# Activations and memory that arrive transposed, at the start of a fused two-block transformer kernel

## The reference

```python
def first_block(x, mem, positions, ...):
    cos, sin = rope_tables(positions, x.dtype)
    mem_n = rmsnorm(mem, g_mem)
    h = rmsnorm(x, g_mix_pre)
    proj = h @ w_in                     # 1024 x 2048
    q, k = proj[..., :512], proj[..., 512:1024]
    v, u = proj[..., 1024:1536], proj[..., 1536:]
    q, k = apply_partial_rope(q, cos, sin), apply_partial_rope(k, cos, sin)
    ...
    pooled = causal_multiscale_pool(u)
    po = jnp.einsum('bsgc,gcd->bsgd', pooled, w_pool) * pool_scale
    ...
    kv = mem_n @ w_xkv                  # cross attention's keys and values

def rmsnorm(x, g):
    return x * lax.rsqrt(jnp.mean(x * x, axis=-1, keepdims=True) + EPS) * g
```

## Time and profile before

| | |
|---|---|
| median of three runs | 1021.13 us (1020.99 to 1021.32) |
| the profiled execution | 1022.37 us, its span 1019.8 us |
| TensorE busy | 1008.9 us, 99% of the span |
| VectorE, ScalarE, GpSimd busy | 761.3 us (75%), 539.2 us (53%), 31.8 us (3%) |
| chain that ended last | TensorE 99%, ScalarE 1% |
| DMA | 183.41 MB, mean 180 GB/s; in the first 45 us some 420 GB/s |

### The profile page before, as it was taken

The page is one execution under the profiler, slowest core; times in us unless marked ns, Lnnn a source line. Parts: engine busy times, 40 slices in busy tenths (PEclk is TensorE's granted clock), DMA queues, the critical chain, the costliest instruction groups (busy, mean ns, idle before and its releaser), DMA issues.

```text
span 1019.8 us, 17235 instructions
## 1 busy us (share of the span) xinstructions
PE 1008.9 (99%) x6914; PEld 905.6 (89%) x6914; DVE 761.3 (75%) x1041; ACT 539.2 (53%) x757; POOL 31.8 (3%) x49
## 2 busy tenths in 40 slices
PE   8999999999999999999999999999999999999997
PEld 7999899898888889998888888889999988888885
DVE  6888587698887457897788888447788869888632
ACT  6876485574544346865464544336534365454431
POOL 1100000000000001000000000001000100000000
PEclk9999999999999999999999999999999999999999
DMA  9833554266555546443345555555434237555521
GB/s 342 349 135 134 197 198 152 86 226 209 205 185 188 204 165 269 176 157 126 125 165 206 203 177 197 206 181 208 166 130 166 84 129 248 201 197 178 201 83 42
DMA packets 27293, 183.41 MB, mean 180 GB/s; under 512 B 3200, under 2 KB 3472, under 8 KB 6112
## 3 DMA queue, kind: packets, MB, share of 16 engines
q1 hardware_dynamic: 25056, 175.01, 48.0%
q0 software_dynamic: 1744, 7.16, 1.9%
q10 hardware_dynamic: 432, 0.37, 0.1%
HBM read 181.48 MB, written 1.05 MB: 179 GB/s over the span
## 4 chain that ended last, share of the span: by engine, by line
PE 99%; ACT 1%; DVE 0%; issue 0%; ACTq 0%
PE GT L1918 11%; PE D L1918 11%; PE GT L1881 10%; PE GT L1882 9%; PE GT L1883 9%; PE D L1881 8%; PE D L1883 8%; PE D L1882 8%; PE GT L1924 6%; PE D L1924 5%; PE D L2652 1%; PE GT L2088 1%; PE GT L2146 1%; PE D L2510 1%; PE GT L2525 1%; PE GT L2107 1%
## 5 line engine op out<-in xcount | busy, mean ns | idle before, releaser
L1033 DVE TENSOR_TENSOR s_wlo<-s_raw,s_whi 128x2048 fp32r<-128x2048 f32 (+1 forms) x164 | 355.5, 2170 | 97.4 <-ACT s_whi L516 95.8
L516 ACT ACTIVATE s_whi<-s_raw 128x2048 fp32r<-128x2048 f32 (+1 forms) x164 | 298.0, 1820 | 140.5 <-PE D L1883 86.1
L1918 PE MATMUL GT<-s_x,s_whi 128*128 128x512 f32 x512 | 124.4, 390 | 0.0
L1918 PE MATMUL D<-s_x,s_whi 128*128 128x512 f32 x480 | 116.4, 390 | 0.0
L1918 PEld LDWEIGHTS GT<-s_x,s_whi 128*128 128x128 f32 x512 | 93.6, 188 | 17.3
L1881 PE MATMUL D<-s_whi,s_hTh 128*128 128x512 f32 x264 | 103.0, 390 | 0.0
L1883 PE MATMUL D<-s_whi,s_hTl 128*128 128x512 f32 x264 | 102.7, 389 | 0.0
L1882 PE MATMUL D<-s_wlo,s_hTh 128*128 128x512 f32 x264 | 102.7, 389 | 0.0
L1918 PEld LDWEIGHTS D<-s_x,s_whi 128*128 128x128 f32 x480 | 87.8, 188 | 16.3
L1881 PE MATMUL GT<-s_x,s_whi 128*128 128x256 f32 x336 | 94.6, 282 | 0.0
L1883 PE MATMUL GT<-s_x,s_wlo 128*128 128x256 f32 x336 | 93.4, 278 | 0.0
(11 more groups left out here) (409 smaller groups left out, 1788.6 us busy)
## 6 DMA issues: line engine op xcount, KB each, us to landing
s_raw<-in_stream SPq DMA_DIRECT2D x164, 1024.0 KB, 4.8
s_gb<-in_rows POOLq DMA_DIRECT2D x4, 512.0 KB, 4.1
s_xn<-in_x SPq DMA_DIRECT2D x2, 512.0 KB, 4.6
s_raw<-in_stream SPq DMA_DIRECT2D x4, 256.0 KB, 6.6
s_y<-in_mem POOLq DMA_DIRECT2D x1, 1024.0 KB, 10.2
s_w<-in_cmpw POOLq DMA_DIRECT2D x1, 1024.0 KB, 10.9
s_poolm<-in_poolm POOLq DMA_DIRECT2D x1, 768.0 KB, 12.1
s_retd<-in_retm POOLq DMA_DIRECT2D x1, 768.0 KB, 5.2
```

The source lines that it names most:

```text
L516: nc.scalar.activation(high(u, n), raw[:, u % RING, 0:n], ACT.Copy)\
L1033: nc.vector.tensor_tensor(low(u, n), raw[:, u % RING, 0:n], high(u, n), ALU.subtract)\
L1918: return nc.tensor.matmul(o[:, f, :], high_block(u, kt, f), x2[:, kt, :], start=start, stop=stop)
```

## The change

x and the memory are given to the program a second time, transposed and laid out as the kernel needs them (`xT`, `memT`: feature on the partition, eight blocks of 256 tokens). The natural ones are still loaded, for the squares and the residual.

- SP's queue: x transposed in three pieces (two blocks, two blocks, four blocks of features), each followed by the part of unit 0 that belongs to it; then unit 1 in two halves, unit 2, the constants in one piece, natural x, unit 3. ScalarE's queue loads only the gains.
- `raw_transposes` is gone: ScalarE and VectorE read the loaded `xraw` (it lies in `y`). One copy on ScalarE of one column of the cleared tile stands ahead. The squares of x move behind the split of unit 2.
- `early_unit` serves units 1, 2 and 3; unit 1 can begin on its first half. Units 2 and 3 are accumulated in banks D0 and D1. The spread of rstd (two matmuls) moves from behind unit 1 to behind unit 3.
- GpSimd: the memory goes into `vx`, and `memT`, one more MB, into `y`, when the high part of unit 3 is ready (before: of unit 4).
- `mem_transposes` is replaced by `mem_rstd`: two matmuls that spread the memory's rstd. VectorE multiplies `memT` by it, now after the low part of unit 8 instead of ahead of the tables.
- The angles are reduced once; the cosine is taken as the sine of pi/2 less the size of the reduced angle.

```diff
+PIECES = ((0, 1), (1, 2), (2, 4))
+PIECE_OF = (0, 1, 2, 2)
...
+        xraw = y[:].rearrange("p t n -> p (t n)").rearrange("p (k n) -> p k n", k=KT)
+        memT = y[:].rearrange("p t (k n) -> p (t k) n", n=S)
+            return (G[0], G[1], DB[0], DB[1])[u]
...
-            for t in range(NT):
-                sp.dma_start(xn[:, t, :], x_in[t * P:(t + 1) * P, :]).then_inc(sem(f"x_in{t}"), 16)
-            for i in range(4):
-                sp.dma_start(raw[:, 0, 512 * i:512 * i + 512], stream[0, :, 512 * i:512 * i + 512])\
+            for i, (a, b) in enumerate(PIECES):
+                sp.dma_start(xraw[:, 2 * a:2 * b, :], xT_in[:, 2 * a:2 * b, :]).then_inc(sem(f"xT_in{i}"), 16)
+                sp.dma_start(raw[:, 0, 512 * a:512 * b], stream[0, :, 512 * a:512 * b])\
                     .then_inc(sem(f"first_in{i}"), 16)
             for j in range(1, RING):
-                sp.dma_start(raw[:, j, :], stream[j, :, :]).then_inc(landed[j], 16)
+                if j == 3:
+                    for t in range(NT):
+                        sp.dma_start(xn[:, t, :], x_in[t * P:(t + 1) * P, :]).then_inc(sem("x_in"), 16)
                 if j == 1:
-                    sp.dma_start(cst[:, CONST_FIRST:], consts_in[:, CONST_FIRST:]).then_inc(sem("cst_in"), 16)
+                    sp.dma_start(raw[:, 1, 0:UNIT // 2], stream[1, :, 0:UNIT // 2]).then_inc(sem("second_in"), 16)
+                    sp.dma_start(raw[:, 1, UNIT // 2:UNIT], stream[1, :, UNIT // 2:UNIT]).then_inc(landed[1], 16)
+                else:
+                    sp.dma_start(raw[:, j, :], stream[j, :, :]).then_inc(landed[j], 16)
+                if j == 2:
+                    sp.dma_start(cst[:], consts_in).then_inc(sem("cst_in"), 16)
...
-            power("x0.0")
-            power("x0.1")
-
-            pool.wait_ge(sem("norm_sq"), 4)
-            pool.wait_ge(hi_ready, 5)
-            pool.dma_start(y[:], mem_in.rearrange("(t p) d -> p t d", p=P)).then_inc(sem("mem_in"), 16)
-            pool.dma_start(poolm[:], poolm_in).then_inc(sem("poolm_in"), 16)
-            pool.dma_start(wpool, wpool_in).then_inc(sem("wpool_in"), 16)
+            pool.wait_ge(sem("cst_in"), 16)
+            power("x0.0")
+            power("x0.1")
+
+            pool.wait_ge(hi_ready, 4)
+            pool.dma_start(vx[:], mem_in.rearrange("(t p) d -> p t d", p=P)).then_inc(sem("mem_in"), 16)
+            pool.dma_start(memT[:], memT_in).then_inc(sem("memT_in"), 16)
+            pool.dma_start(poolm[:], poolm_in).then_inc(sem("pool_in"), 16)
+            pool.dma_start(wpool, wpool_in).then_inc(sem("pool_in"), 16)
+            pool.wait_ge(unit_done, 1)
             pool.dma_start(gb[:], rows_in[0, :].partition_broadcast(P)).then_inc(sem("gb_in"), 16)
...
+            def mem_hi():
+
+                for kt in range(KT):
+                    if kt % 4 == 0:
+                        act.wait_ge(sem("mem_scaled"), kt // 4 + 1)
+                    nc.scalar.activation(memTh[:, kt, :], memT[:, kt, :], ACT.Copy, scale=gain("g_mem", kt))\
+                        .then_inc(sem("norm_hi"), 1)
...
-            norm_squares(0, xn, lambda c: chunk(y, c), parts=range(2))
+            act.wait_ge(sem("warm_in"), 1)
+            nc.scalar.activation(small[:, 0:1], gb[:, 0:1], ACT.Copy)
             for i in range(4):
-                norm_hi(0, xTh, (2 * i, 2 * i + 1))
-                act.wait_ge(sem(f"first_in{i}"), 16)
+                act.wait_ge(sem(f"xT_in{PIECE_OF[i]}"), 16)
+                for kt in (2 * i, 2 * i + 1):
+                    nc.scalar.activation(xTh[:, kt, :], xraw[:, kt, :], ACT.Copy, scale=gain("g_mix_pre", kt))\
+                        .then_inc(sem("norm_hi"), 1)
+                act.wait_ge(sem(f"first_in{PIECE_OF[i]}"), 16)
                 nc.scalar.activation(whi[:, 0, 512 * i:512 * i + 512], raw[:, 0, 512 * i:512 * i + 512],
                                      ACT.Copy).then_inc(sem("first_hi") if i < 3 else hi_ready, 1)
-            for j in range(1, 4):
-                split(j)
+            act.wait_ge(sem("second_in"), 16)
+            nc.scalar.activation(whi[:, 1, 0:UNIT // 2], raw[:, 1, 0:UNIT // 2], ACT.Copy).then_inc(sem("first_hi"), 1)
+            act.wait_ge(landed[1], 16)
+            nc.scalar.activation(whi[:, 1, UNIT // 2:UNIT], raw[:, 1, UNIT // 2:UNIT], ACT.Copy).then_inc(hi_ready, 1)
+            split(2)
+            norm_squares(0, xn, lambda c: x_scratch[:, c, :], parts=range(2))
+            split(3)
...
             act.wait_ge(sem("mem_in"), 16)
-            mem_scratch = kxT[:].rearrange("p (c k) n -> p c (k n)", c=4)
-            norm_squares(1, y, lambda c: mem_scratch[:, c, :])
+            norm_squares(1, vx, lambda c: x_scratch[:, c, :])
...
-            norm_hi(1, memTh)
+            mem_hi()
...
-            def mem_scaled(t):
-
-                dve.wait_ge(rstd_ready, pow_at(f"mem.{t}") + 1)
-                nc.vector.tensor_scalar(y[:, t, :], y[:, t, :], rstd[:, POW_COL[f"mem.{t}"]], None, ALU.mult)\
+            def mem_scaled(b):
+
+                if b == 0:
+                    dve.wait_ge(sem("memT_in"), 16)
+                    dve.wait_ge(sem("norm_tr"), 4)
+                part = memT[:, 4 * b:4 * b + 4, :]
+                nc.vector.tensor_tensor(part, part, same_rows(DB[2][:, 0:S], 4), ALU.mult)\
                     .then_inc(sem("mem_scaled"), 1)
+            def mem_lo():
...
+                    nc.vector.scalar_tensor_tensor(memTl[:, kt, :], memT[:, kt, :], gain("g_mem", kt), memTh[:, kt, :],
+                                                   ALU.mult, ALU.subtract).then_inc(sem("xT_ready"), 1)
...
-            dve.wait_ge(sem("x_in1"), 16)
             dve.wait_ge(sem("gains_in"), 16)
             for i in range(4):
-                norm_lo(0, xTh, xTl, (2 * i, 2 * i + 1))
+                dve.wait_ge(sem(f"xT_in{PIECE_OF[i]}"), 16)
+                dve.wait_ge(sem("norm_hi"), 2 * i + 2)
+                for kt in (2 * i, 2 * i + 1):
+                    nc.vector.scalar_tensor_tensor(xTl[:, kt, :], xraw[:, kt, :], gain("g_mix_pre", kt),
+                                                   xTh[:, kt, :], ALU.mult, ALU.subtract)\
+                        .then_inc(sem("xT_ready"), 1)
...
+            dve.wait_ge(sem("x_in"), 32)
...
-            angle(sinT, 0.0, 0.0)
+            link(nc.vector.tensor_scalar(turns, ang, 1.0 / two_pi, magic, ALU.mult, ALU.add))
+            link(nc.vector.tensor_scalar(turns, turns, -magic, None, ALU.add))
+            for c in (c1, c2, c3):
+                link(nc.vector.scalar_tensor_tensor(ang, turns, -c, ang, ALU.mult, ALU.add))
+            link(nc.vector.tensor_scalar(sinT[:], ang, 3.1415925, -3.1415925, ALU.min, ALU.max))
+            link(nc.vector.scalar_tensor_tensor(cosT[:], sinT[:], -1.0, sinT[:], ALU.mult, ALU.max))
+            nc.vector.tensor_scalar(cosT[:], cosT[:], math.pi / 2, None, ALU.subtract).then_inc(sem("angles"), 1)
...
-            dve.wait_ge(sem("angles"), 1)
-            angle(cosT, math.pi / 2, 0.25)
             norm_mean(1, "mem", 0)
             norm_mean(1, "mem", 1)
-            mem_scaled(0)
-            mem_scaled(1)
...
                 split(u0 + 4 + j + RING)
+                if j == 0:
+                    mem_scaled(0)
+                    mem_scaled(1)
                 if j == 1:
-                    norm_lo(1, memTh, memTl)
+                    mem_lo()
...
-            def second_unit(u):
+            def early_unit(u):
 
                 hi, lo = (w(u).rearrange("p (k n) -> p k n", k=KT) for w in (high, low))
-                o = G[bank(u)]
-                pe.wait_ge(hi_ready, u + 1)
+                o = first_bank(u)
+                if u == 1:
+                    pe.wait_ge(sem("first_hi"), 4)
+                else:
+                    pe.wait_ge(hi_ready, u + 1)
                 for t in range(NT):
                     for kt in range(KT):
+                        if u == 1 and t == 0 and kt == KT // 2:
+                            pe.wait_ge(hi_ready, u + 1)
...
-            def mem_transposes():
-
+            def mem_rstd():
+
+                pe.wait_ge(rstd_ready, pow_at("mem.1") + 1)
                 for t in range(NT):
-                    pe.wait_ge(sem("mem_scaled"), t + 1)
-                    for kt in range(KT):
-                        c = S * (kt % 2) + P * t
-                        ins = nc.tensor.transpose(o[kt // 2][:, c:c + P], y[:, t, P * kt:P * kt + P], ident)
-                        if t == NT - 1 and kt % 2:
-                            ins.then_inc(sem("norm_tr"), 1)
+                    ins = nc.tensor.matmul(DB[2][:, P * t:P * t + P], rstd[:, POW_COL[f"mem.{t}"]].broadcast_to([P, P]),
+                                           ident, start=True, stop=True)
+                ins.then_inc(sem("norm_tr"), 4)
...
-            raw_transposes()
             u0 = BASE["in"]
             first_unit()
-            second_unit(u0 + 1)
+            for u in range(u0 + 1, u0 + 4):
+                early_unit(u)
```

(6 more changed lines are left out.)

70 lines of the change are left out of this document (27 added, 43 removed).

## The result

The changed kernel is slower, by 0.2%. Its median is 1023.17 us (1022.04 to 1028.90, 20 runs) against 1021.59 us for the kernel before (1020.48 to 1023.21, 20 runs). The ratio is 1.0022, with an interval of 1.0015 to 1.0029. The forecast was 1018.0 us and a range to 1020.4. The profiled execution took 1022.72 us with a span of 1019.7, so it is one of the faster ones. The profiled execution of the kernel before took 1022.37 with a span of 1019.8, which is slower than its own median. Side by side the two profiles show 0.1 us of span; the medians of the times are 1.6 us apart.

The account below looks back on a forecast made before the run. TensorE's order of matmuls was taken to bound the kernel; 2.1 us at the start plus 1.3 us on the memory, less a 0.3 us wait, saved 3.1 us from the 1021.13 median: 1018.0 us, range 1016.8 to 1020.4.

Parts of the forecast that it names:

- The bound: Whole span: TensorE busy 1008.9 of 1019.8 us; loses only if a buffer, bank or operand is not ready earlier.
- Units 2 and 3: Early units in banks D0 and D1: no added wait, zero cost; unit 3's later landing hidden with 1.8 us of cover.
- The two spreads: Memory's rstd on TensorE: 0.37 us added for 1.66 us of transposes removed, a gain of 1.3 us.
- The two scalings of VectorE: Memory scaled by rstd in PSUM, taken as 1.2 us each instead of 0.75, hidden behind unit 6.
- The chain from the split of unit 7 to the free bank: ScalarE's unbroken chain ahead of unit 6, 8.83 us plus 0.74 for VectorE's product: 9.57 us.
- The wait: Ahead of unit 6: unit 4's bank free at 43.3, TensorE ready at 43.0, so it stands 0.3 us.
- where both queues had work, SP's had 66.8% of the engines and GpSimd's the rest: Queue share read from the trace before, applied to unit 7 loading beside the memory, now loaded twice.
- At that share 1.05 MB take 3.8 us: Unit 7's transfer behind unit 6, which ends at about 28.7; landing at 33.5 to 33.9, taken as 33.7.
- rival (b): Queues share half and half: unit 7 moves 5.0 us, lands at 34.8; saving 2.0 us, 1019.1; chance 0.15.
- I take 9.5: Landing of unit 0's last half, between 8.9 and 10.1; unit 0 ends at 13.9 instead of 16.01, gain 2.1 us.
- Rival (c), slow products at the start: Last 20 products of unit 0 at half rate, ending 2.4 us later; 1.0 us saved, 1020.1; chance 0.12.
- The sum: Up to unit 6: 3.4 us gained less 0.3 us of waiting, a saving of 3.1 us.

Follow-up runs that it names:

- e11: e6 with the last 512 KB pieces of x and unit 0 cut, giving four pairs of 256 KB; 1019.51 us, ratio 0.9979.
- e18: e11 with the memory's part undone: one copy, loaded row by row, scaled on VectorE, transposed by TensorE; 1020.12 us, ratio 0.9987.
- e12: e6 with x and unit 0 in two halves each, 512 KB per piece, rows of 4 KB; 1019.72 us, ratio 0.9978.
- e9: Kernel before the change with four 128x1024 copies on VectorE ahead of unit 4's cosine product; 1023.75 us, ratio 1.0021.
- e1: The changed kernel again, no edit; 1023.24 us, ratio 1.0026.
- e15: The changed kernel again, no edit, another profiled execution; 1022.25 us.
- e6: Changed kernel with the late posting of e5 and the sines ahead of unit 7's high part as in e3; 1021.34 us, ratio 0.9997.
- e2: Changed kernel with seven unused products of 128 columns in the two gaps of unit 0; 1025.38 us, ratio 1.0041.
- e4: Changed kernel with the edits of e2 and e3 together; 1022.09 us, ratio 1.0007.
- e16: The same kernel as in e15, another profiled execution; 1025.11 us.
- e13: Changed kernel with only the last pair of 512 KB pieces cut into two pairs of 256 KB; 1024.71 us, ratio 1.0038.
- e14: e7 with the first pieces cut into four pairs of 256 KB; 1022.97 us, ratio 1.0017.
- e5: Changed kernel with transposed memory, pooling matrix and w_pool posted only after unit 7's high part is begun; 1021.82 us, ratio 1.0004.
- e10: e6 with 22 unread products of 256 columns filling the gaps of unit 0; 1026.29 us, 4.95 above e6.
- e17: Changed kernel with e5's late posting and e11's four pairs of 256 KB, sines left behind unit 7's high part; 1021.03 us, ratio 0.9995.
- e3: Changed kernel with only the two sines on ScalarE moved ahead of unit 7's split; 1021.51 us, ratio 0.9999.
- e7: Changed kernel with the memory's part undone, its start and fewer angle steps kept; 1022.26 us, ratio 1.0009.

## Why the prediction was wrong

**What held.** The bound: the loss lies in front of TensorE, in operands that come late (in the profile). The first product was forecast at 6.25 and came at 6.12. Units 2 and 3, the evacuation of unit 0 and the halved unit 1 were hidden. The two spreads took 0.36 us in place of 1.66 (e11, e18). The two scalings of VectorE took 2.35 us together against 2.4 in the forecast, and were hidden. The chain from the split of unit 7 to the free bank was 9.57 us by the forecast and 9.62 in the profile (36.16 to 45.78). The wait came where it was said; its size was wrong.

**The step that failed: "where both queues had work, SP's had 66.8% of the engines and GpSimd's the rest", and with it "At that share 1.05 MB take 3.8 us".** The share was right for the kernel before. It came of equal counts of packets, 68 and 64, when GpSimd's queue moved the memory in packets of 4 KB and SyncE's a unit in 8 KB. The transposed memory comes in packets of 8 KB, and then the counts are equal again (92 and 91) and so are the shares, 49.9 and 49.6%. Unit 7 moved for 5.3 us (the splits that waited for units 6 and 7 begin at 30.82 and 36.16), not 3.8. It also began late: unit 3 landed at 22.5 instead of 21.5, so unit 7 was issued at 26.94 instead of 25.8, and unit 6 landed at 30.8, not 28.7, with 81.9% of the engines at GpSimd's queue from 28 to 30 us. The forecast's own terms don't meet here: 28.7 and 3.8 are 32.5, not 33.5 to 33.9. Unit 7 landed at 36.14, and with the chain behind it the bank was free 2.5 us after the forecast. That was rival (b), and worse than it: I had priced it at 34.8. The Trainium skill, "DMA: Bandwidth & Descriptors", section "Queues, rings and completion order", says each engine takes turns between its queues by packets. The trace agrees from 31 us on (153 and 150 packets to 36 us) and not from 28 to 30 (29 and 161).

**The term that was mis-sized: "I take 9.5" for the last half of unit 0.** It came to 10.5; the bound above was 10.1. The rate was 239 to 264 GB/s from 4 to 8 us, a longer dip than the one of the earlier trace rows, and I had taken the middle between a dip and none. Unit 0 ended 0.9 us earlier than in the profile of before, not 2.1. Smaller last pieces (e11, 14.25) or two halves (e12, 14.15) would have ended it 0.9 to 1.0 us earlier still.

**The base that was wrong.** 16.01, 46.39 and all milestones of before came from one execution whose span was 1.1 us above the median of before (1019.8 and 1018.7). The forecast saw the 1.24 us in the time and took the saving from the median, but it took the milestones as they stood. In e9 the same code starts unit 1 0.87 us earlier, at 15.14, since all transposes of x run at the fast rate. Which start is the usual one no run tells; if it is e9's, the start gained nothing where the forecast had 2.1 us.

**Rival (c), slow products at the start.** It came true in part of the executions: in two of the changed kernel's four profiles (e1, e15) the granted clock fell to 0.5 at the start for some 3.4 us, behind waits of 1.90 and 1.93. I had looked at the first 20 products only, and argued from one gap of 0.95 us. The 1.00 that the views print for the first microseconds is no reading: the trace of before has its first record of the clock at 7.42 us and e9's at 5.50, and the transposes' 421 and 272 ns fit that. In this kernel it is not what was lost: TensorE waits at unit 6 anyway, and in the lower group the nine runs with a clock of 0.997 or more have a mean span of 1019.4, the ten below it 1019.8. Where nothing waits at unit 6 it does cost: in e6 the six runs with 0.997 or more have 1017.6, the five below 1019.3. At unit 6, the three profiles whose two waits add up to 2.6 us or more (e2, e4, e16) have a low stretch behind them, and of six with 1.7 to 2.1 us (the first, e5, e9, e13, e14, e15) one has. The kernel before has no such stretch in its profile, nor in e9's. That the removed transposes had kept the clock up is not shown; the filled starts of e2, e4 and e10 have no low stretch ahead of 45 us in their profiles, which is for it, but three profiles are few. The Trainium skill, "TensorE: Matmul & The Clock Gate", section "Part 1: The HAM clock gate", says an idle array is clocked at 1.2 GHz and only a busy one at 2.4; the trace agrees on the two levels (0.5 and 1.00), and the waits of 1.65 and 0.93 us in the first profile brought no fall.

**The sum.** By the forecast's own chain the landing at 36.14 leaves 0.5 us of the 3.1: unit 6 at 45.93 instead of 46.39. Against e9's 45.35 it is a loss of 0.6. The median span of the lower group is 1019.5, 0.8 above before's 1018.7, which fits that loss; the 13 runs of the upper group, some 3 us higher, lift the median of all 32 to 1020.2; and 0.3 us come outside the span. The upper group ends when the transposed memory is posted late (e5, e17) and also when the sines alone stand ahead (e3), so it hangs on the chain behind unit 7's landing; what makes the 3 us in it is shown for e16 alone. From 8 to 36 us the engines are never idle, so each added megabyte, 2.5 us at 0.42 MB/us, delays what lands behind it.

## What to carry to other kernels

Where the DMA engines are full, an operand loaded a second time to save an engine's work is paid by whatever lands last in that stretch; follow the bytes to the end of the full stretch, not to the next unit. Read a queue's share with its packets: here two busy queues mostly moved equal counts, so a second queue with rows twice as long took half of the engines instead of a third. Post what is needed late behind what is needed early. Work that is taken from TensorE ahead of a wait lengthens the wait and may cost the clock as well; the kernels with several short waits at the start (e11, e12) were the fastest. And take the milestones of before from more than one execution when the gain is as small as the spread of the start.

## What the runs showed that was not expected

**Two rhythms of the same matmuls.** Products of 256 columns at a granted clock of 1.00 start 117.8 or 113.3 ns apart, in long stretches. Near 700 us, the changed kernel and the kernel before:

```profile
700.05 0.28 PE L1919 MATMUL GT<-s_x,s_whi 128*128 128x256 f32 x1
700.17 0.28 PE L1920 MATMUL GT<-s_x,s_wlo 128*128 128x256 f32 x1
700.29 0.28 PE L1918 MATMUL GT<-s_x,s_whi 128*128 128x256 f32 x1
```

```profile
702.05 0.28 PE L1882 MATMUL GT<-s_x,s_whi 128*128 128x256 f32 x1
702.16 0.28 PE L1883 MATMUL GT<-s_x,s_wlo 128*128 128x256 f32 x1
702.27 0.28 PE L1881 MATMUL GT<-s_x,s_whi 128*128 128x256 f32 x1
```

The kernel before changed to the faster one at about 700 us, the changed kernel at 720; its profile was 1.0 us ahead until then and lost 0.8 of it in these 20 us. Earlier it is the other way round: it changed at 32 us, the kernel before for good only at about 75. What sets the rhythm wasn't found, and a part of the 1.1 us between the profile of before and its median may be this.

**Time outside the span.** Time less span is 2.57 us for the kernel before and 2.89 for the changed one (means). Every kernel that loads the transposed memory has 2.7 to 3.2, those without have 2.2 to 2.6 (e7, e9, e14, e18). That is 0.3 of the 1.6 us, and between e11 and e18 0.45, over a third of what e11 gains in the span. No run tells the cause.

**Filler products** of plain f32 take 0.43 us for 256 columns (two matmuls of 0.216 in the trace, e10) where those of fp32r take 0.118, at the same granted clock.

**Open.** Why unit 7 lands 1.5 us later in e16, the one profile of the upper group, wasn't found: in e16 SyncE's queue had 45.1% from 28 to 38 us against 46.1% in the first profile, and its transfer was issued at the same time (26.95 and 26.94). How much of each run's excess is lost clock could only be read for profiled executions.
